# Expert loop of a mixture layer: another order of the operand splits, of the loads, and of the release of v and w tiles

## The chip, the cores and the metric

The kernel runs on one core of one Trainium2 chip. The metric is the time of one execution on the device in microseconds (us). Beside TensorE (PE) the core has VectorE (DVE), ScalarE (ACT), GpSimd (POOL) and SyncE (SP), which here only issues loads and stores. Each engine runs its own list of instructions in order; they wait for each other on counting semaphores.

## The reference

An encoder of two layers for 512 tokens of width 1024. A layer is a token mixer, a cross attention and a retrieval feed-forward (peer_ffn), which is the part that the change touches. It picks, for each token and each of 8 heads, 16 out of 16384 experts; an expert is one row of peer_u and one of peer_v:

```python
u = peer_u[eb]
a = jax.nn.gelu(jnp.einsum('thkd,td->thk', u, xb).astype(jnp.float32))
wgt = (a * gb).astype(xb.dtype)
return jnp.einsum('thk,thkd->td', wgt, peer_v[eb])
```

## The kernel before

For three of the four 128-token tiles (DENSE, DTOK = 384 tokens) the kernel does not gather. It computes every expert densely, with a gate that is zero for experts that a token did not choose. The 16384 experts are 128 tiles of 128; `expert_stage` goes over them in 32 groups of GROUP = 4 (e = 0 to 3). The program's text is expanded once and run for each of the two layers. The last token tile does gather: GpSimd fetches 128 rows of peer_u and of peer_v at a time, four of each per group, and VectorE does their products (row_product, row_output).

All dense products are done as three float32r matmuls (`mm3`, lines 123 to 125): high part by high part, low by high and high by low. So each tile of weights or gates has to be split: ScalarE copies it to the rounded high part ("hi", u_hi, v_hi, w_hi) and VectorE subtracts that from the raw tile (the low part "lo", u_lo, v_lo, w_lo).

One group, by engine:

- TensorE: for each e the first product (24 matmuls over 8 chunks of the width, tile A0 to A3 in this text) of u tile e with the 384 tokens, into bank 2 + e % 2. It waits for the low part (`ulo`) and for the gelu that freed the bank (`ge`). Then the second product, twice 36 matmuls: half 0 gives columns 0 to 511, half 1 columns 512 to 1023, in each half e = 0 to 3, and for each e three token tiles; it sums over all four experts in six banks, and counts `om` as each is done.
- ScalarE, for each e: v_hi e, u_hi of the next but one tile, gelu e, w_hi e. v_hi 0 of a group waits until the second product of the group before is wholly done (`om`, line 1971). After the four, the gelu of the four row products.
- VectorE, for each e: v_lo e, u_lo, multiplication by the gates (`exp_w<-exp_w,exp_gates`, line 2027), w_lo e. Then four row products (L1999), the row weights, two row outputs (L2007), three additions of the output banks of half 0 to the residual (L2014), two row outputs, three additions of half 1.
- SyncE, for each e: the load of u tile n + 2 once u_lo n is done, of v tile n + 2 once v_lo n is done, of the gates n + 2 once the multiplication n is done (line 1884, `ahead`). The raw buffers ur, vr and gt hold two tiles each (slot e % 2). uh and ul too hold two tiles, vh, vl, wh and wl hold the four of a group. In the first two groups stores of gates of the last block stand between the loads (`store_gates`).

A semaphore's wait in the same list holds back all that stands behind it on that engine. That is what sets the order of the work here: nothing is scheduled by a program, all is written out.

Of the kernel before, what the change touches and what calls it, by code (L numbers as in the profile page):

```python
# [18 lines left out]
ALU = mybir.AluOpType  # L19
# [22 lines left out]
GROUP = 4  # L42
# [1762 lines left out]
def expert_stage(nc, res, U, V, last_block, SL, u_rows, v_rows, l):  # L1805
# [7 lines left out]
    with Stage(nc, "exp") as st:  # L1813
# [31 lines left out]
        ad = st.sem("output_bank_added")  # L1845
        rd = st.sem("row_products_summed")
# [7 lines left out]
        def _(sp):  # L1854
# [29 lines left out]
            def ahead(g, e, last):  # L1884
                n = g * GROUP + e
                sp.wait_ge(ulo, n + 1)
                load_u(0 if last and e >= GROUP - 2 else n + 2, e % 2)
                if not (last and e >= GROUP - 2):
                    sp.wait_ge(vlo, n + 1)
                    load_v(n + 2, e % 2)  # L1890
                    sp.wait_ge(wo, n + 3)
                    load_g(n + 2, e % 2)

            for n in range(FIRST):
                if n == GROUP:

                    sp.wait_ge(g_out, 32)
                ahead(n // GROUP, n % GROUP, False)
                store_gates(n + 1)
            sp.wait_ge(g_out, 16 * (FIRST + 1))  # L1900
            with sp.Fori(FIRST // GROUP, NG - 1) as g:
                for e in range(GROUP):
                    ahead(g, e, False)
            for e in range(GROUP):
                ahead(NG - 1, e, True)
# [21 lines left out]
        def _(pe):  # L1927
            pe.sem_inc(am, 1)
            pe.sem_inc(om, 1)
            with pe.Fori(0, NG) as g:  # L1930
# [9 lines left out]
                for half in range(2):  # L1940
                    cols = slice(half * CHUNK, (half + 1) * CHUNK)
                    for e in range(GROUP):
# [3 lines left out]
                        for t in range(DENSE):  # L1946
# [5 lines left out]
                            if e == GROUP - 1:  # L1952
                                i.then_inc(om, 1)

        @b.scalar
        def _(act):
# [7 lines left out]
            u_hi(1, 1)  # L1964
            with act.Fori(0, NG) as g:
                for e in range(GROUP):
                    n = g * GROUP + e
                    act.wait_ge(v_in[e % 2], g * 32 + (e // 2) * 16 + 16)
                    if e == 0:

                        act.wait_ge(om, g * NO + 1)
                    act.copy(vh[:, e], vr[:, e % 2]).then_inc(vho, 1)  # L1972
                    if e:
                        act.wait_ge(am, n + 1)
                        u_hi(n + 1, (e + 1) % 2)
                    act.wait_ge(am, n + 2)
                    act.wait_ge(wlo, n + 1)
                    act.activation(w[:, e % 2], PS[:, 2 + e % 2, 0:DTOK], ACT.Gelu_apprx_tanh).then_inc(ge, 1)  # L1978
                    act.wait_ge(wo, n + 3)
                    act.copy(wh[:, e], w[:, e % 2]).then_inc(who, 1)  # L1980
# [328 lines left out]
```

## Time and profile before

| | us |
|---|---|
| median of three runs | 5006.38 |
| lowest, highest | 5004.93, 5008.29 |
| the profiled execution, its own time | 5007.78 |
| its span | 5006.0 |
| TensorE busy | 4198.0 (84%) |
| VectorE busy | 3155.8 (63%) |
| ScalarE busy | 1736.2 (35%) |

The page gives busy time and the costliest groups of instructions with the idle time of the engine in front of them and what ended it. The expert loops of the two layers run from about 1285 to 2500 us and from about 3775 to 4990 us of the span. Within them the work repeats from group to group, so a timeline of one group, with start times in us from the span's start, is the most telling view; the windows show the granted TensorE clock (1.00 is 2.4 GHz, 0.50 is 1.2 GHz) and what the transfer engines move.

### The profile page before, as it was taken

The page shows a single profiled execution, that of the slowest core. Times are in us where ns is not written, and L with a number is a line of the kernel's source. Part 1 is how long each engine was busy: PE and PEld are TensorE (multiplying, and loading weights), DVE is VectorE, ACT ScalarE, POOL GpSimd, SP SyncE. Part 2 cuts the span into 40 slices and gives each one's busy share as a digit, 9 for nine tenths or more (in the row PEclk, how much of TensorE's full clock was granted, in tenths as well). Part 3 has the DMA queues.
Part 4 walks back from the last instruction along what each step waited for, and adds up shares of the span by engine and source line. Part 5 has one row for each costly group of instructions (what it writes and reads, how often), then busy time and mean ns, then how long its engine had stood idle before and what let it go on. Part 6 is the DMA issues. An engine that isn't in the chain of part 4 may idle for free. (4 is left out here: it accounts for less than half of the span.)

```text
span 5006.0 us, 64200 instructions
## 1 busy us (share of the span) xinstructions
PE 4198.0 (84%) x21706; PEld 3734.1 (75%) x21706; DVE 3155.8 (63%) x5125; ACT 1736.2 (35%) x2506; POOL 1391.9 (28%) x992
## 2 busy tenths in 40 slices
PE   8869798646799999999897797886467999999997
PEld 6669677546688888888776796775466888888887
DVE  3464334599677777777735543336896777777776
ACT  2242222109543343333322322221094334334333
POOL 0143101155322322322201531112553232232231
PEclk9989899879899999999998898998798999999999
DMA  3100212105877777777531003120058777777775
GB/s 116 47 9 1 101 59 72 34 1 131 249 261 244 242 251 242 251 246 243 198 104 42 9 1 110 64 67 26 1 140 270 247 245 251 244 247 249 239 249 196
DMA packets 458568, 750.34 MB, mean 150 GB/s; under 512 B 241232, under 2 KB 278864, under 8 KB 458192
## 3 DMA queue, kind: packets, MB, share of 16 engines
q1 hardware_dynamic: 384720, 480.40, 29.5%
q0 software_dynamic: 73728, 268.47, 15.8%
q8 instruction: 60, 0.98, 0.1%
q14 instruction: 60, 0.49, 0.0%
HBM read 696.35 MB, written 52.43 MB: 150 GB/s over the span
## 5 line engine op out<-in xcount | busy, mean ns | idle before, releaser
L123 PE MATMUL banks<-act_hi,exp_uT_hi 128*128 128x384 f32 x2048 | 742.8, 363 | 183.6 <-DVE exp_uT_lo L1994 183.6
L1913 POOL DMA_INDIRECT exp_u_gathered<-in_peer_u,row_experts x256 | 390.3, 1525 | 1601.3 <-DVE exp_row_a L1999 1532.3
L124 PE MATMUL banks<-act_hi,exp_uT_lo 128*128 128x384 f32 x2048 | 732.7, 358 | 0.0
L125 PE MATMUL banks<-act_lo,exp_uT_hi 128*128 128x384 f32 x2048 | 732.4, 358 | 0.0
L124 PE MATMUL banks<-exp_v_hi,exp_w_lo 128*128 128x512 f32 x1536 | 598.4, 390 | 0.0
L123 PE MATMUL banks<-exp_v_hi,exp_w_hi 128*128 128x512 f32 x1536 | 598.1, 389 | 0.0
L125 PE MATMUL banks<-exp_v_lo,exp_w_hi 128*128 128x512 f32 x1536 | 597.7, 389 | 0.0
L123 PEld LDWEIGHTS banks<-act_hi,exp_uT_hi 128*128 128x128 f32 x2048 | 416.2, 203 | 208.1 <-DVE exp_uT_lo L1994 205.6
L124 PEld LDWEIGHTS banks<-act_hi,exp_uT_lo 128*128 128x128 f32 x2048 | 416.4, 203 | 2.4
L125 PEld LDWEIGHTS banks<-act_lo,exp_uT_hi 128*128 128x128 f32 x2048 | 415.2, 203 | 0.0
L1972 ACT CAST exp_v_hi<-exp_v_raw 128x1024 fp32r<-128x1024 f32 x256 | 268.0, 1047 | 355.1 <-PE banks L125 354.7
L2027 DVE TENSOR_TENSOR exp_w<-exp_w,exp_gates 128x384 f32<-128x384 f32 x256 | 142.0, 555 | 357.3 <-ACT exp_w L1978 335.2
L1994 DVE TENSOR_TENSOR exp_uT_lo<-exp_uT_raw,exp_uT_hi 128x1024 fp32r<-128x1024 f32 x260 | 317.2, 1220 | 72.5 <-ACT exp_uT_hi L1961 72.3
L2022 DVE TENSOR_TENSOR exp_v_lo<-exp_v_raw,exp_v_hi 128x1024 fp32r<-128x1024 f32 x256 | 313.0, 1223 | 78.1 <-ACT exp_v_hi L1972 78.1
L2007 DVE SCALAR_TENSOR_TENSOR residual<-exp_v_gathered,exp_row_w,residual 128x1024 f32<-128x1024 f32 x256 | 328.2, 1282 | 15.6
L125 PEld LDWEIGHTS banks<-exp_v_lo,exp_w_hi 128*128 128x128 f32 x1536 | 288.4, 188 | 60.4
L123 PEld LDWEIGHTS banks<-exp_v_hi,exp_w_hi 128*128 128x128 f32 x1536 | 288.3, 188 | 58.2
L124 PEld LDWEIGHTS banks<-exp_v_hi,exp_w_lo 128*128 128x128 f32 x1536 | 288.3, 188 | 57.7
L1913 POOL DMA_INDIRECT exp_v_gathered<-in_peer_v,row_experts x256 | 285.4, 1115 | 84.3 <-issue 75.9
L1725 DVE TENSOR_TENSOR gate_one_hots<-slot_keys,iota 128x1024 f32<-128x1024 f32 x192 | 296.8, 1619 | 3.0 <-DVE row_experts L1689 1.7
L1999 DVE CUSTOM_DVE_ANT_0 exp_u_gathered<-exp_u_gathered,rows 128x1024 f32<-128x1024 f32 x256 | 298.5, 1222 | 0.0
L1748 PE MATMUL banks<-gate_one_hots,gate_gated_one_hots 128*128 128x128 f32 x1536 | 205.7, 289 | 101.7 <-POOL gate_gated_one_hots L1735 79.8
(386 smaller groups left out, 8295.8 us busy)
## 6 DMA issues: line engine op xcount, KB each, us to landing
exp_uT_raw<-in_peer_uT SPq DMA_DIRECT2D x260, 512.0 KB, 4.2
exp_v_raw<-in_peer_v SPq DMA_DIRECT2D x256, 512.0 KB, 4.3
exp_gates<-dense_gates SPq DMA_DIRECT2D x256, 192.0 KB, 2.7
win_project_raw<-in_w_in SPq DMA_DIRECT2D x32, 1024.0 KB, 5.5
dense_gates<-gate_block SPq DMA_DIRECT2D x6, 4096.0 KB, 20.7
wkv_project_raw<-in_w_xkv SPq DMA_DIRECT2D x16, 1024.0 KB, 5.0
wpq_project_raw<-in_peer_wq SPq DMA_DIRECT2D x16, 1024.0 KB, 5.1
dense_gates<-last_gates SPq DMA_DIRECT2D x4, 4096.0 KB, 20.7
```

What stands on the lines that cost most here:

```text
L123: pe.matmul(out, lhs[0], rhs[0], start=first, stop=False)
L124: pe.matmul(out, lhs[1], rhs[0], start=False, stop=False)
L125: return pe.matmul(out, lhs[0], rhs[1], start=False, stop=last)
L1725: dve.tensor_tensor(oh[:, q], SL.idx[:, :, bass.ds(first(it, q), SUB)][:, :, :, None].broadcast_to(shape), res.iota[:, None, None, :].broa ...
L1748: i = pe.matmul(PS[:, q, k * P:(k + 1) * P], gh[:, q, k, :], oh[:, q, 0, k, :], start=True, stop=True)
L1913: pool.indirect_dma_start(out, None, table, bass.IndirectOffsetOnAxis(SL.row_idx[:, slot:slot + 1], 0)).then_inc(done, 16)
L1972: act.copy(vh[:, e], vr[:, e % 2]).then_inc(vho, 1)
L1994: dve.tensor_tensor(ul[:, slot], ur[:, slot], uh[:, slot].bitcast(F32), ALU.subtract).then_inc(ulo, 1)
L1999: dve.tensor_tensor_reduce(out=gu[:, e], in0=gu[:, e], in1=SL.rows[:], scale=1.0, scalar=0.0, op0=ALU.mult, op1=ALU.add, accum_out=ra[:, e ...
L2007: dve.scalar_tensor_tensor(out=X[:, DENSE, :], in0=gv[:, e], scalar=rw[:, e:e + 1], in1=X[:, DENSE, :], op0=ALU.mult, op1=ALU.add).then_in ...
L2022: dve.tensor_tensor(vl[:, e], vr[:, e % 2], vh[:, e].bitcast(F32), ALU.subtract).then_inc(vlo, 1)
L2027: dve.tensor_tensor(w[:, e % 2], w[:, e % 2], gt[:, e % 2], ALU.mult).then_inc(wo, 1)
```

## The change

Five things are moved; no computation is added or left out.

1. ScalarE and VectorE do the u parts of tile n + 2 as the first thing after tile n of the first product is done, in front of the gelu.
2. TensorE counts a new semaphore `vw` when expert e (0 to 2) is done in the second half of the second product. ScalarE's v_hi 0, 1 and 2 wait for that instead of for the end of the whole product; v_hi 3 waits for the end. v_hi 0 and 1 move in front of the group's first gelu, v_hi 2 and 3 stand between gelu 0 and w_hi 0 and between gelu 1 and w_hi 1.
3. w_hi and w_lo of an expert follow the v parts of a later one.
4. SyncE's loads are listed in another order, and the loads of u tiles 2 and 3 stand in front of the loop.
5. On VectorE the first row product stands between the multiplication by gates and w_lo of expert 2.

The diff, cut to the lists and functions:

```diff
+        vw = st.sem("v_and_w_used")
...
-            def ahead(g, e, last):
-                n = g * GROUP + e
+            def u_after(n, slot, dummy=False):
                 sp.wait_ge(ulo, n + 1)
-                load_u(0 if last and e >= GROUP - 2 else n + 2, e % 2)
-                if not (last and e >= GROUP - 2):
-                    sp.wait_ge(vlo, n + 1)
-                    load_v(n + 2, e % 2)
-                    sp.wait_ge(wo, n + 3)
-                    load_g(n + 2, e % 2)
-
-            for n in range(FIRST):
-                if n == GROUP:
+                load_u(0 if dummy else n + 2, slot)
+
+            def v_after(n, slot):
+                sp.wait_ge(vlo, n + 1)
+                load_v(n + 2, slot)
+
+            def g_after(n, slot):
+                sp.wait_ge(wo, n + 3)
+                load_g(n + 2, slot)
+
+            def ahead(g, last, stores):
+                n = g * GROUP
+                v_after(n + 0, 0)
+                v_after(n + 1, 1)
+                for e in range(GROUP):
+                    if e == GROUP - 1 and not last:
+                        g_after(n + e, e % 2)
+                    if not last or e < 2:
+                        u_after(n + e + 2, e % 2, last)
+                    if e < GROUP - 1 and (not last or e < 2):
+                        g_after(n + e, e % 2)
+                    if e + 2 < GROUP and (not last or e + 2 < 2):
+                        v_after(n + e + 2, (e + 2) % 2)
+                    if stores:
+                        store_gates(n + e + 1)
+
+            u_after(0, 0)
+            u_after(1, 1)
+            for g in range(FIRST // GROUP):
+                if g == 1:
 
                     sp.wait_ge(g_out, 32)
-                ahead(n // GROUP, n % GROUP, False)
-                store_gates(n + 1)
+                ahead(g, False, True)
...
-                for e in range(GROUP):
-                    ahead(g, e, False)
-            for e in range(GROUP):
-                ahead(NG - 1, e, True)
+                ahead(g, False, False)
+            ahead(NG - 1, True, False)
...
+            pe.sem_inc(vw, GROUP - 1)
...
@@ -1951,6 +1970,8 @@
                                     (vh[:, e, cols], vl[:, e, cols]), e == 0, e == GROUP - 1)
                             if e == GROUP - 1:
                                 i.then_inc(om, 1)
+                            elif half == 1 and t == DENSE - 1:
+                                i.then_inc(vw, 1)
...
+            def v_hi(g, e):
+                act.wait_ge(v_in[e % 2], g * 32 + (e // 2) * 16 + 16)
+                act.copy(vh[:, e], vr[:, e % 2]).then_inc(vho, 1)
+
+            def gelu(n, e):
+                act.wait_ge(am, n + 2)
+                act.wait_ge(wlo, n + 1)
+                act.activation(w[:, e % 2], PS[:, 2 + e % 2, 0:DTOK], ACT.Gelu_apprx_tanh).then_inc(ge, 1)
+
+            def w_hi(n, e):
+                act.wait_ge(wo, n + 3)
+                act.copy(wh[:, e], w[:, e % 2]).then_inc(who, 1)
+
             with act.Fori(0, NG) as g:
-                for e in range(GROUP):
-                    n = g * GROUP + e
-                    act.wait_ge(v_in[e % 2], g * 32 + (e // 2) * 16 + 16)
+                n = g * GROUP
+                for e in range(2):
+                    act.wait_ge(vw, g * (GROUP - 1) + e + 1)
+                    v_hi(g, e)
+                for e in range(GROUP - 1):
+                    act.wait_ge(am, n + e + 2)
+                    u_hi(n + e + 2, e % 2)
+                    gelu(n + e, e)
                     if e == 0:
-
+                        act.wait_ge(vw, g * (GROUP - 1) + GROUP - 1)
+                        v_hi(g, 2)
+                    if e == 1:
                         act.wait_ge(om, g * NO + 1)
-                    act.copy(vh[:, e], vr[:, e % 2]).then_inc(vho, 1)
-                    if e:
-                        act.wait_ge(am, n + 1)
-                        u_hi(n + 1, (e + 1) % 2)
-                    act.wait_ge(am, n + 2)
-                    act.wait_ge(wlo, n + 1)
-                    act.activation(w[:, e % 2], PS[:, 2 + e % 2, 0:DTOK], ACT.Gelu_apprx_tanh).then_inc(ge, 1)
-                    act.wait_ge(wo, n + 3)
-                    act.copy(wh[:, e], w[:, e % 2]).then_inc(who, 1)
-                act.wait_ge(am, g * GROUP + GROUP + 1)
-                u_hi(g * GROUP + GROUP + 1, 1)
-                act.wait_ge(rd, g * GROUP + GROUP)
+                        v_hi(g, 3)
+                    w_hi(n + e, e)
+                gelu(n + GROUP - 1, GROUP - 1)
+                u_hi(n + GROUP + 1, 1)
+                w_hi(n + GROUP - 1, GROUP - 1)
+                act.wait_ge(rd, n + GROUP)
...
+            def v_lo(n, e):
+                dve.wait_ge(vho, n + 1)
+                dve.tensor_tensor(vl[:, e], vr[:, e % 2], vh[:, e].bitcast(F32), ALU.subtract).then_inc(vlo, 1)
+
+            def gated(g, n, e):
+                dve.wait_ge(ge, n + 3)
+                dve.wait_ge(g_in[e % 2], g * 32 + (e // 2) * 16 + 16)
+                dve.tensor_tensor(w[:, e % 2], w[:, e % 2], gt[:, e % 2], ALU.mult).then_inc(wo, 1)
+
+            def w_lo(n, e):
+                dve.wait_ge(who, n + 1)
+                dve.tensor_tensor(wl[:, e], w[:, e % 2], wh[:, e].bitcast(F32), ALU.subtract).then_inc(wlo, 1)
+
             with dve.Fori(0, NG) as g:
-                for e in range(GROUP):
-                    n = g * GROUP + e
-                    dve.wait_ge(vho, n + 1)
-                    dve.tensor_tensor(vl[:, e], vr[:, e % 2], vh[:, e].bitcast(F32), ALU.subtract).then_inc(vlo, 1)
-                    if e:
-                        u_lo(n + 1, (e + 1) % 2)
-                    dve.wait_ge(ge, n + 3)
-                    dve.wait_ge(g_in[e % 2], g * 32 + (e // 2) * 16 + 16)
-                    dve.tensor_tensor(w[:, e % 2], w[:, e % 2], gt[:, e % 2], ALU.mult).then_inc(wo, 1)
-                    dve.wait_ge(who, n + 1)
-                    dve.tensor_tensor(wl[:, e], w[:, e % 2], wh[:, e].bitcast(F32), ALU.subtract).then_inc(wlo, 1)
-                u_lo(g * GROUP + GROUP + 1, 1)
-                row_product(g, 0)
-                row_product(g, 1)
-                row_product(g, 2)
-                row_product(g, 3)
+                n = g * GROUP
+                v_lo(n, 0)
+                v_lo(n + 1, 1)
+                for e in range(GROUP - 1):
+                    u_lo(n + e + 2, e % 2)
+                    gated(g, n + e, e)
+                    if e < 2:
+                        v_lo(n + e + 2, e + 2)
+                    else:
+                        row_product(g, 0)
+                    w_lo(n + e, e)
+                gated(g, n + GROUP - 1, GROUP - 1)
+                u_lo(n + GROUP + 1, 1)
+                w_lo(n + GROUP - 1, GROUP - 1)
+                for e in range(1, GROUP):
+                    row_product(g, e)
```

What stands in a row on ScalarE (exp_uT is u, exp_v is v, exp_w the gelu's output). At the beginning of a group's gelu 0, before:

```order
L1978 ACT_TABLE_LOAD
L1978 ACTIVATE exp_w<-banks 128x384
...
L1980 CAST exp_w_hi<-exp_w 128x384
L1972 CAST exp_v_hi<-exp_v_raw 128x1024
...
L1961 CAST exp_uT_hi<-exp_uT_raw 128x1024
```

The same place on ScalarE after the change, from the two v_hi that now open the group:

```order
L1988 CAST exp_v_hi<-exp_v_raw 128x1024
L2002 REGISTER_ALU
L1988 CAST exp_v_hi<-exp_v_raw 128x1024
...
L1982 CAST exp_uT_hi<-exp_uT_raw 128x1024
L1992 REGISTER_ALU
L1993 ACT_TABLE_LOAD
L1993 ACTIVATE exp_w<-banks 128x384
...
L1988 CAST exp_v_hi<-exp_v_raw 128x1024
L1996 REGISTER_ALU
L1997 CAST exp_w_hi<-exp_w 128x384
L1982 CAST exp_uT_hi<-exp_uT_raw 128x1024
```

The u copy of tile 2 stood fifth, behind the table load, the gelu, w_hi 0 and v_hi 1; it stands before the table load now, and v_hi 2 and w_hi 0 stand between gelu 0 and the u copy of tile 3.

VectorE at the beginning of a group, before:

```order
L2022 TENSOR_TENSOR exp_v_lo<-exp_v_raw,exp_v_hi 128x1024
L2025 REGISTER_ALU
L2026 ISA
L2027 TENSOR_TENSOR exp_w<-exp_w,exp_gates 128x384
L2029 TENSOR_TENSOR exp_w_lo<-exp_w,exp_w_hi 128x384
L2021 REGISTER_ALU
L2022 TENSOR_TENSOR exp_v_lo<-exp_v_raw,exp_v_hi 128x1024
L1994 TENSOR_TENSOR exp_uT_lo<-exp_uT_raw,exp_uT_hi 128x1024
```

And after:

```order
L2055 TENSOR_TENSOR exp_v_lo<-exp_v_raw,exp_v_hi 128x1024
L2028 REGISTER_ALU
L2029 TENSOR_TENSOR exp_uT_lo<-exp_uT_raw,exp_uT_hi 128x1024
L2059 ISA
L2060 TENSOR_TENSOR exp_w<-exp_w,exp_gates 128x384
L2055 TENSOR_TENSOR exp_v_lo<-exp_v_raw,exp_v_hi 128x1024
L2064 TENSOR_TENSOR exp_w_lo<-exp_w,exp_w_hi 128x384
L2028 REGISTER_ALU
L2029 TENSOR_TENSOR exp_uT_lo<-exp_uT_raw,exp_uT_hi 128x1024
```

The first row here is v_lo 1. u_lo 2 follows it at once, where it stood behind the multiplication, w_lo 0 and v_lo 1; u_lo 3 stands behind v_lo 2 and w_lo 0.

SyncE in one pass of the loop (the ISA row ahead of a load is its wait), after the change; before it was u, v, gates four times:

```order
L1860 DMA exp_v_raw<-in_peer_v 128x1024
L1860 ISA
L1860 DMA exp_v_raw<-in_peer_v 128x1024
L1857 ISA
L1857 DMA exp_uT_raw<-in_peer_uT 128x1024
L1863 ISA
L1863 DMA exp_gates<-dense_gates 128x384
L1860 ISA
L1860 DMA exp_v_raw<-in_peer_v 128x1024
```

Two v loads, on v_lo 0 and v_lo 1, now open the pass; the u loads of tiles 2 and 3 that stood there have gone to the end of the pass before and ahead of the loop.

## Rows read from the trace of the kernel before

**Rows 1.** The page: busy time; costliest group (busy, mean ns, idle before, releaser).
```profile
PE 4198.0 (84%) x21706; PEld 3734.1 (75%) x21706; DVE 3155.8 (63%) x5125; ACT 1736.2 (35%) x2506; POOL 1391.9 (28%) x992
...
L123 PE MATMUL banks<-act_hi,exp_uT_hi 128*128 128x384 f32 x2048 | 742.8, 363 | 183.6 <-DVE exp_uT_lo L1994 183.6
```

**Rows 2.** ScalarE timeline (start us, us, operation): row gelu, groups 0 and 31.
```profile
1334.87 0.20 ACT L1984 ACTIVATE exp_row_gelu<-exp_row_a 128x4 f32<-128x4 f32 x1 [5.87 <-DVE exp_row_a L1999]
...
2487.13 0.20 ACT L1984 ACTIVATE exp_row_gelu<-exp_row_a 128x4 f32<-128x4 f32 x1 [5.87 <-DVE exp_row_a L1999]
...
3826.92 0.21 ACT L1984 ACTIVATE exp_row_gelu<-exp_row_a 128x4 f32<-128x4 f32 x1 [5.87 <-DVE exp_row_a L1999]
...
4979.24 0.21 ACT L1984 ACTIVATE exp_row_gelu<-exp_row_a 128x4 f32<-128x4 f32 x1 [5.87 <-DVE exp_row_a L1999]
```

**Rows 3.** TensorE timeline of one group [idle before <-releaser].
```profile
1808.48 0.40 PE L123 MATMUL banks<-exp_v_hi,exp_w_hi 128*128 128x512 f32 x1
...
1824.84 0.34 PE L123 MATMUL banks<-act_hi,exp_uT_hi 128*128 128x384 f32 x1
...
1833.15 0.33 PE L125 MATMUL banks<-act_lo,exp_uT_hi 128*128 128x384 f32 x1
...
1835.76 0.44 PE L123 MATMUL banks<-act_hi,exp_uT_hi 128*128 128x384 f32 x1 [2.28 <-DVE exp_uT_lo L1994]
```

**Rows 4.** Windows, TensorE alone: window, length, busy, granted clock, DMA share, GB/s.
```profile
1838.40:1839.40 1.00, 1.00 (x5) 0.50 0.85 317
```

**Rows 5.** Windows: busy by engine (instructions), granted clock, DMA share, GB/s.
```profile
40.00:160.00 120.00, 120.00 (x515) 96.50 (x514) 40.56 (x34) 19.59 (x11) 0.00 (x0) 1.00 0.30 96
1340.00:1420.00 80.00, 75.43 (x367) 68.95 (x366) 59.77 (x76) 30.55 (x40) 25.04 (x20) 0.96 0.86 283
1420.00:2480.00 1060.00, 993.78 (x4782) 904.48 (x4781) 770.08 (x993) 413.41 (x547) 296.09 (x224) 0.96 0.72 246
```

**Rows 6.** ScalarE timeline: a table load at the layer's start, then one group's beginning.
```profile
1290.42 1.04 ACT L1961 CAST exp_uT_hi<-exp_uT_raw 128x1024 fp32r<-128x1024 f32 x1 [2.38 <-DMA exp_uT_raw<-in_peer_uT]
1291.48 1.28 ACT L1972 ACT_TABLE_LOAD   x1
...
1825.04 1.05 ACT L1972 CAST exp_v_hi<-exp_v_raw 128x1024 fp32r<-128x1024 f32 x1 [5.95 <-PE banks L125]
1829.34 1.28 ACT L1978 ACT_TABLE_LOAD   x1 [3.25 <-PE banks L125]
1830.64 0.49 ACT L1978 ACTIVATE exp_w<-banks 128x384 f32<-128x384 f32 x1
...
1832.27 1.05 ACT L1972 CAST exp_v_hi<-exp_v_raw 128x1024 fp32r<-128x1024 f32 x1
1833.22 1.03 ACT L1961 CAST exp_uT_hi<-exp_uT_raw 128x1024 fp32r<-128x1024 f32 x1
```

**Rows 7.** VectorE timeline, end of one group and beginning of the next.
```profile
1811.51 1.23 DVE L1994 TENSOR_TENSOR exp_uT_lo<-exp_uT_raw,exp_uT_hi 128x1024 fp32r<-128x1024 f32 x1 [0.40 <-ACT exp_uT_hi L1961]
...
1824.86 1.88 DVE L2014 TENSOR_TENSOR residual<-banks,residual 128x512 f32<-128x512 f32 x3
1826.66 1.22 DVE L2022 TENSOR_TENSOR exp_v_lo<-exp_v_raw,exp_v_hi 128x1024 fp32r<-128x1024 f32 x1
...
1833.35 1.22 DVE L2022 TENSOR_TENSOR exp_v_lo<-exp_v_raw,exp_v_hi 128x1024 fp32r<-128x1024 f32 x1 [0.39 <-ACT exp_v_hi L1972]
1834.49 1.22 DVE L1994 TENSOR_TENSOR exp_uT_lo<-exp_uT_raw,exp_uT_hi 128x1024 fp32r<-128x1024 f32 x1
```

**Rows 8.** SyncE queue timeline: the group's first v load.
```profile
1828.10 0.33 SPq L1859 DMA_DIRECT2D exp_v_raw<-in_peer_v  x1
```

**Rows 9.** Landing: that load; v loads, 1420 to 2430; u loads, 1340 to 1420.
```profile
DMA to landing us min/median/max: 5.3/5.3/5.3
...
DMA to landing us min/median/max: 3.1/4.3/5.6
...
DMA to landing us min/median/max: 3.3/5.7/8.1
```

## Prediction

> **What bounds the kernel now.** I read the page first. TensorE is busy 84% of the span, and in front of the first product of the expert loop it has waited 183.6 us, all for VectorE's u_lo at L1994 [rows 1]. So the loop is held by TensorE, with a hole that belongs to the u tiles.
>
> Next, the length of a group. The row gelu stands once per group of four experts; from group 0 to group 31 it moves 2487.13 - 1334.87 = 1152.26 us in layer 1 and 1152.32 us in layer 2, so 31 groups take 37.17 us each [rows 2].
>
> Next, what TensorE needs. Its timeline shows the second product from 1808.48 to 1824.84, without a hole: 16.36 us. Then two tiles of the first product, whose last matmul starts at 1833.15; with one spacing of 0.177 us (8.48 us for 48 matmuls) they take 8.48 us, 4.24 us a tile. The third tile starts only at 1835.76, after 2.28 us of waiting for u_lo [rows 3]. Four tiles and the second product at this pace are 4 x 4.24 + 16.36 = 33.32 us. The remaining 37.17 - 33.32 = 3.85 us are the wait (2.3 to 2.5 us) and a spell at half clock that follows it: in 1838.4 to 1839.4 the granted clock is 0.50, 1.2 instead of 2.4 GHz [rows 4]. Over the loop it averages 0.96, while in 120 us of projection in which TensorE never idles it is 1.00 [rows 5]. I therefore count the spell as a consequence of the wait.
>
> **Why u is late before.** In each group's timelines, tile A0 ends 4.24 after the group's start and ScalarE reacts at 4.50 (1829.34). But it then does the table load, gelu 0, w_hi 0, v_hi 1 and only then u_hi 2, at 1833.22, 8.4 us after the group's start [rows 6]. u_lo 2 starts at 1834.49 behind v_lo 1, and TensorE goes on 1.27 later [rows 7, 3].
>
> **The change part by part.** I walk the new orders with t = 0 at a group's first matmul, and TensorE at full clock: A0 to A3 start at 0, 4.24, 8.48, 12.72, the second product at 16.96; its second half at 25.14, and that half's experts 0, 1, 2 end at 27.2, 29.2, 31.3.
>
> 1. u first (releases tile A2). u_hi 2 at 4.50. u_lo starts 1.08 after a hi copy (v_hi 1832.27 to v_lo 1833.35, [rows 6, 7]): 5.58; TensorE may go at 5.58 + 1.27 = 6.85. A2 is due at 8.48: 1.6 us spare, the wait of 2.3 is gone. What is late next? A2 also needs gelu 0 out of its bank. The table load now stands behind u_hi: 4.50 + 1.05 = 5.55, gelu at 5.55 + 1.30 = 6.85 (1829.34 to 1830.64), done 7.34: 1.1 spare.
>
> 2. v_hi 0 and 1 in the preceding group's second half, on their experts' release (27.2 and 29.2), while ScalarE before sits idle until the output is done (5.95 us at 1825.04, [rows 6]). Cost nothing; their table load goes there too. Their lo parts stay behind the last three output additions on VectorE. Those now wait for TensorE: the last bank is done at 33.5, so the third addition starts at 0.25 of the next group and v_lo 0 at 0.85 (an addition takes 1.88 / 3), v_lo 1 at 2.0.
>
> 3. The queue. SP issues the load of v 2 1.44 after v_lo starts (1826.66 to 1828.10, [rows 7, 8]): 2.3. It lands 5.3 later by the single row, 5.6 at most in 1420 to 2430 [rows 9]: 7.6 to 7.9. ScalarE wants it for v_hi 2 behind gelu 0, at 7.25, so v_hi 2 starts at 7.6. Behind it on ScalarE stand w_hi 0 (8.55) and u_hi 3 (9.0; A1 ends at 8.48, seen at 8.74). On VectorE: v_lo 2 at 8.7, w_lo 0 at 9.85, u_lo 3 at 10.4; TensorE may go at 11.7. A3 is due at 12.72: 1.0 spare. This is the tightest place. The load may land up to 6.3 us after its issue before TensorE waits at all. The other loads have more: v 3 is issued at 3.4 and wanted at 10.4; u 4 at 7.0, wanted at 13.0; u 5 at 11.8, wanted at 17.6. The waits in SP's new list (v_lo 0, v_lo 1, u_lo 2, w 0, v_lo 2, u_lo 3, w 1, ...) fulfil in that order, so none is queued behind a later one.
>
> 4. Second half of the loop on VectorE. Before, from the last u_lo (1811.51) to the last addition group (1824.86) is 13.35 us [rows 7]. After, A3 is done at 16.96, gelu 3 starts at 17.2, u_hi 5 at 17.6, u_lo 5, the last, at 18.7; one row product less (1.14, the spacing of 1024-column operations at 1833.35 and 1834.49) and a w_lo more (384 columns, 0.5 as an estimate from that) stand behind it: ready for the last additions at 31.4, when their first bank is done at 32.1. w_lo 3 starts near 19.9 and the second product's expert 3 begins at 23.1. So VectorE has 0.7 us left per group, and no wait for TensorE here.
>
> 5. DMA volume is the same, 9.17 MB a group (sixteen tiles of 512 KB, 192 KB of gates four times): 246 GB/s now at a share of 0.72, 275 GB/s then. In 1340 to 1420, with gate stores beside, the queues carried 283 GB/s at 0.86 [rows 5]. It fits, with little over.
>
> The increments of vw ride on existing matmuls. The added waits are ScalarE's, on counts that are raised before it comes (2.0 us before the group's end at the latest for v_hi 2). I take 0. No row prices a wait that is already met; nothing makes it a gain, and as a loss it has to exceed the 1.0 us of spare of step 3 before TensorE notices: 0.1 us a group, 6 us, is my bound.
>
> **Sum.** 3.85 x 31 = 119.4 us a layer. At the layer's end the last additions end 0.85 us after the last matmul instead of 1.9 (1824.86 + 1.88): 1.1. Group 0 waits for its first gates as before: 0, between -2 and +3. Two layers: 2 x 120.5 = 241 us. The profiled run is 5007.8, 1.4 above the median of 5006.4; 5006.4 - 241 gives 4766 (and 4767 for a profiled one).
>
> **Rivals.**
> (a) A smaller wait takes the old one's place at A2 or A3. What speaks for it: 1.0 and 1.1 us of spare on chains of six steps. The table load now comes right behind a copy, where it was behind an idle wait of 3.25 us. At the layer's start it also stands behind a copy, at 1291.48 after 1290.42 + 1.04, and costs nothing extra [rows 6]. Bounds for an extra drain: 0 by that row, above one more load, 1.28 us, as far as rows go. With the latter gelu 0 is done at 8.62 and A2 waits 0.2 us a group: 62 x 0.2 = 12, 4778; if every such wait brought the slow spell (about 1.6 us) too, 62 x 1.8 = 112, 4878.
> The Trainium skill (ScalarE: Activation LUTs, What ACT_TABLE_LOAD costs) puts a switch of set at about 2.66 us, load and drain together; the trace here has 1.28 and no drain. By the page gelu 0 would end as late as under the upper bound, give or take 0.1 us, and the time would be the one just worked out from rows.
> (b) The queues give out. v 2 lands later than 6.3 us after issue. For it: u loads took up to 8.1 us at 283 GB/s, behind gate stores [rows 9]. Against: the stores are gone after two groups, and the gathers of v rows, which a row output releases, get further from this load: row outputs 2 and 3 ended with the group (1824.86, [rows 7]) and the load came 3.3 later; now they end at 31.4, 1.9 before the group's end, and the load comes at 2.3, so 4.2 later. At 8.1 us A3 is 1.8 late, plus the spell: 62 x 3.4 = 211, 4977.
> (c) The slow spell is not a consequence of the wait: 62 x (3.85 - 2.4) = 90 stay, 4856. Against it stand the 120 us at 1.00.
> (d) Slower than before: v_hi 2 blocks ScalarE, with u_hi 3 behind it. From landings over 6.3 + 3.85 - 1.6 = 8.6 us on (spell included) a group is longer than 37.17; at 9.5 us 62 x 0.9 = 56 more, 5062. No v load took that long in 1420 to 2430.
> (e) The change doesn't do what it says: ScalarE comes late to u_hi 2, for instance held at the loop's top by v_hi 1. Then nothing moves, 5006. Against: by the walk that tile's load is issued 17 us before v_hi 0 wants it (10.2 and 27.2).
>
> **How the numbers follow.** Forecast 0.74; (a) 0.10, (b) 0.05, (c) 0.04, (d) 0.03, (e) 0.04. The forecast is 4766. Its own range, from group 0, the cost of waits and 0.1 us a group, is 4756 to 4776. To leave out no more than 2 in 10, the range takes in (a) and (c): 4756 to 4878. About 0.2% (10 us) is what a measurement can tell from no change. Faster 0.93, same 0.04, slower 0.03.
>
> **What would show it.** The row gelus 33.3 us apart; granted clock 1.00 inside the loop; TensorE's wait for u_lo at the first product below 30 us in all, in the layers' first groups; u_hi 2 at 4.5, u_lo 3 near 10.4; v_hi 2 released by its load, near 7.6; loop at 275 GB/s. Wrong would be: a wait before every fourth tile with v_hi 2 starting beyond 8.6 (b, d); a hole before the third with gelu 0 later than 8 (a); clock dips without holes (c).

## The result, and the profile after

| | before | after |
|---|---|---|
| median, 4 runs each | 5005.66 us | 4765.98 us |
| lowest, highest | 5003.36, 5008.29 | 4762.16, 4767.08 |
| ratio, 95% interval | | 0.952 (0.9503 to 0.9536) |
| span of the profiled execution | 5006.0 | 4764.2 |

The changed kernel is faster by 240 us; 241 were forecast. The page of its profile (busy time, and the costliest group as in [rows 1]: busy, mean ns, idle before, releaser):

```profile
PE 4097.4 (86%) x21706; PEld 3654.1 (77%) x21706; DVE 3147.7 (66%) x5125; ACT 1729.5 (36%) x2506; POOL 1352.9 (28%) x992
...
L123 PE MATMUL banks<-act_hi,exp_uT_hi 128*128 128x384 f32 x2048 | 699.4, 341 | 43.9 <-ACT exp_w L1993 23.9
```

The idle time in front of the first product fell from 183.6 to 43.9 us; 20.0 of it, in 4 waits, is still for u_lo, and the other 23.9 is for the gelu. The mean of one such matmul fell too, from 363 to 341 ns, since the half-clock spells of the steady groups are gone. The window of the loop, as the last of [rows 5] (busy by engine, clock, DMA share, GB/s):

```profile
1420.00:2330.00 910.00, 910.00 (x4589) 832.27 (x4588) 738.22 (x960) 390.24 (x519) 270.76 (x218) 1.00 0.84 276
```

In 910 us TensorE has no hole and is at full clock throughout, while the transfer engines move 276 GB/s where they moved 246.

The timeline of one group follows; its first matmul is at 1807.23, and times into the group count from there. ScalarE:

```profile
1801.36 1.28 ACT L1988 ACT_TABLE_LOAD   x1 [3.48 <-PE banks L125]
1802.65 2.00 ACT L1988 CAST exp_v_hi<-exp_v_raw 128x1024 fp32r<-128x1024 f32 x2
1811.73 1.05 ACT L1982 CAST exp_uT_hi<-exp_uT_raw 128x1024 fp32r<-128x1024 f32 x1 [7.07 <-PE banks L125]
1812.80 1.28 ACT L1993 ACT_TABLE_LOAD   x1
1814.09 0.49 ACT L1993 ACTIVATE exp_w<-banks 128x384 f32<-128x384 f32 x1
1814.48 1.04 ACT L1988 CAST exp_v_hi<-exp_v_raw 128x1024 fp32r<-128x1024 f32 x1
...
1815.89 1.05 ACT L1982 CAST exp_uT_hi<-exp_uT_raw 128x1024 fp32r<-128x1024 f32 x1
```

VectorE in the same group (the last additions of the group before, then v_lo 0 and 1, u_lo 2, u_lo 3, and the last u_lo):

```profile
1806.05 2.05 DVE L2049 TENSOR_TENSOR residual<-banks,residual 128x512 f32<-128x512 f32 x3 [0.78 <-PE banks L125]
1808.02 2.35 DVE L2055 TENSOR_TENSOR exp_v_lo<-exp_v_raw,exp_v_hi 128x1024 fp32r<-128x1024 f32 x2
1812.81 1.23 DVE L2029 TENSOR_TENSOR exp_uT_lo<-exp_uT_raw,exp_uT_hi 128x1024 fp32r<-128x1024 f32 x1 [2.44 <-ACT exp_uT_hi L1982]
...
1817.16 1.22 DVE L2029 TENSOR_TENSOR exp_uT_lo<-exp_uT_raw,exp_uT_hi 128x1024 fp32r<-128x1024 f32 x1
...
1825.83 1.23 DVE L2029 TENSOR_TENSOR exp_uT_lo<-exp_uT_raw,exp_uT_hi 128x1024 fp32r<-128x1024 f32 x1 [0.38 <-ACT exp_uT_hi L1982]
```

The queue's two v loads there, and how long the first of them took to land:

```profile
1809.49 1.49 SPq L1860 DMA_DIRECT2D exp_v_raw<-in_peer_v  x2
...
DMA to landing us min/median/max: 4.8/4.8/4.8
```

u_hi 2 starts at 4.50 us into the group and the table load stands behind it; the gelu follows 1.29 after the load's start. v_hi 2 comes at 7.25, straight behind the gelu, with no wait for its load.

ScalarE's row gelus, as in [rows 2], of group 3 and of group 31 of the first layer:

```profile
1431.15 0.20 ACT L2019 ACTIVATE exp_row_gelu<-exp_row_a 128x4 f32<-128x4 f32 x1 [4.78 <-DVE exp_row_a L2034]
...
2364.11 0.20 ACT L2019 ACTIVATE exp_row_gelu<-exp_row_a 128x4 f32<-128x4 f32 x1 [4.78 <-DVE exp_row_a L2034]
```

From 1431.15 to 2364.11 there are 28 steps of 33.32 us. Group 2 is longer: from its first matmul to group 3's it takes 37.16 us (35.10 in the second layer). The waits in each layer that are left behind its first matmul are at A2 of group 0 and at A3 of group 2. TensorE in the first layer (A2 of group 0, then group 2's first matmul, its A3, and group 3's first matmul):

```profile
1310.64 0.66 PE L123 MATMUL banks<-act_hi,exp_uT_hi 128*128 128x384 f32 x1 [11.57 <-ACT exp_w L1993]
...
1370.21 0.34 PE L123 MATMUL banks<-act_hi,exp_uT_hi 128*128 128x384 f32 x1
...
1385.14 0.53 PE L123 MATMUL banks<-act_hi,exp_uT_hi 128*128 128x384 f32 x1 [2.05 <-DVE exp_uT_lo L2029]
...
1407.37 0.34 PE L123 MATMUL banks<-act_hi,exp_uT_hi 128*128 128x384 f32 x1
```

### The profile page after: what moved, and what is told of

Read it like the earlier page. It is cut to its first block and busy times, and to the rows that moved or that the text cites. A ratio compares the mean times of both kernels' runs of the same rounds, so it can differ in the third digit from the quotient of the medians.

```text
span 4764.2 us, 64232 instructions
## 1 busy us (share of the span) xinstructions
PE 4097.4 (86%) x21706; PEld 3654.1 (77%) x21706; DVE 3147.7 (66%) x5125; ACT 1729.5 (36%) x2506; POOL 1352.9 (28%) x992
## 5 line engine op out<-in xcount | busy, mean ns | idle before, releaser
L123 PE MATMUL banks<-act_hi,exp_uT_hi 128*128 128x384 f32 x2048 | 699.4, 341 | 43.9 <-ACT exp_w L1993 23.9
L1931 POOL DMA_INDIRECT exp_u_gathered<-in_peer_u,row_experts x256 | 324.0, 1266 | 1357.1 <-DVE exp_row_a L2034 1305.3
L124 PE MATMUL banks<-act_hi,exp_uT_lo 128*128 128x384 f32 x2048 | 697.9, 341 | 0.0
L125 PE MATMUL banks<-act_lo,exp_uT_hi 128*128 128x384 f32 x2048 | 697.8, 341 | 0.0
L1982 ACT CAST exp_uT_hi<-exp_uT_raw 128x1024 fp32r<-128x1024 f32 x260 | 272.8, 1049 | 531.4 <-PE banks L125 488.0
L123 PEld LDWEIGHTS banks<-act_hi,exp_uT_hi 128*128 128x128 f32 x2048 | 388.0, 189 | 48.1 <-DVE exp_uT_lo L2029 45.7
L124 PEld LDWEIGHTS banks<-act_hi,exp_uT_lo 128*128 128x128 f32 x2048 | 388.0, 189 | 2.4
L125 PEld LDWEIGHTS banks<-act_lo,exp_uT_hi 128*128 128x128 f32 x2048 | 387.9, 189 | 0.0
L1931 POOL DMA_INDIRECT exp_v_gathered<-in_peer_v,row_experts x256 | 312.2, 1220 | 132.2 <-DVE residual L2042 72.4
L2049 DVE TENSOR_TENSOR residual<-banks,residual 128x512 f32<-128x512 f32 x384 | 251.5, 687 | 48.3 <-PE banks L125 48.3
```

The lines of the kernel that those rows point to most:

```text
L123: pe.matmul(out, lhs[0], rhs[0], start=first, stop=False)
L124: pe.matmul(out, lhs[1], rhs[0], start=False, stop=False)
L125: return pe.matmul(out, lhs[0], rhs[1], start=False, stop=last)
L1931: pool.indirect_dma_start(out, None, table, bass.IndirectOffsetOnAxis(SL.row_idx[:, slot:slot + 1], 0)).then_inc(done, 16)
L1982: act.copy(uh[:, slot], ur[:, slot]).then_inc(uho, 1)
L2049: dve.tensor_tensor(x, PS[:, OUT[half][t], :], x, ALU.add).then_inc(ad, 1)
```

## The experiments

Every kernel here is measured beside the kernel before on the same chip. e1 to e5 are one execution each, and the time of before is given with each; e8, e9 and e10 are medians of 4 or 5.

### Which part carries the gain

**e1: the tile-by-tile release undone.** The changed kernel, but v_hi 0, 1 and 2 wait for the whole second product.

```diff
             with act.Fori(0, NG) as g:
                 n = g * GROUP
+                act.wait_ge(om, g * NO + 1)
                 for e in range(2):
-                    act.wait_ge(vw, g * (GROUP - 1) + e + 1)
                     v_hi(g, e)
```

> The changed kernel with the tile-by-tile release undone: v_hi 0, 1 and 2 wait for the whole second product again, u parts first and the new queue stay. My theory (the release only buys landing time for the load of v 2): v_hi 0 begins 1.5 us into the group behind its table load instead of 4.6 us before it, v_lo 0 at 2.6, the load of v 2 is issued at 4.0 instead of 2.3 and lands near 8.7 to 9.3; u_lo 3 starts at 11.5 to 12.0 and the fourth tile of the first product waits 0.1 to 0.6 us. Group of 33.4 to 33.9 us, 4772 to 4803 us in all, up to 100 us more if such a short wait brings the half-clock spell. Rival (the release is what carries the gain): a group of over 36 us, 4930 us or more.

Measured: 4767.56 us (before 5008.51), groups of 33.32. Nothing is lost, and TensorE waits nowhere between 1420 and 2300. The rows of one group, with its first matmul at 1806.63; ScalarE, then the queue, then the landing of the first load:

```profile
1808.18 2.00 ACT L1984 CAST exp_v_hi<-exp_v_raw 128x1024 fp32r<-128x1024 f32 x2
1811.13 1.05 ACT L1978 CAST exp_uT_hi<-exp_uT_raw 128x1024 fp32r<-128x1024 f32 x1 [0.96 <-PE banks L125]
...
1813.97 1.05 ACT L1984 CAST exp_v_hi<-exp_v_raw 128x1024 fp32r<-128x1024 f32 x1
...
1810.74 1.49 SPq L1859 DMA_DIRECT2D exp_v_raw<-in_peer_v  x2
...
DMA to landing us min/median/max: 3.2/3.2/3.2
```

The v copies fit between the group's start and u_hi 2, with 0.96 us to spare. The v load leaves 4.11 us into the group instead of 2.26, but it lands in 3.2 us instead of 4.8, at 7.3; and v_hi 2 isn't late. That landing is what the expectation had wrong: it took 4.7 to 5.3 us for it, and so a short wait at A3 and 4772 us at least. The release brings nothing that a single execution can tell (1.6 us between this one and the changed kernel's median).

**e2: the old queue.** The changed kernel with SyncE's list of before (u, v, gates four times).

```diff
-            def ahead(g, last, stores):
-                n = g * GROUP
-                v_after(n + 0, 0)
-                v_after(n + 1, 1)
...
+            def ahead(g, e, last):
+                n = g * GROUP + e
+                sp.wait_ge(ulo, n + 1)
+                load_u(0 if last and e >= GROUP - 2 else n + 2, e % 2)
+                if not (last and e >= GROUP - 2):
+                    sp.wait_ge(vlo, n + 1)
+                    load_v(n + 2, e % 2)
+                    sp.wait_ge(wo, n + 3)
+                    load_g(n + 2, e % 2)
```

> The changed kernel with the old queue alone: SyncE again issues u, v, gates for each expert in turn, so the load of u 3 stands behind the gates' wait of expert 0. My theory (the queue is needed, since the u parts now want their tiles earlier): u 3 is issued at 8.7 us of the group instead of in the group before and lands at 13, the fourth tile waits 2.6 us; u 4 and u 5 come late too and hold w_hi 3, which the second product's last expert waits for by some 4 us. Group of 40 to 44 us, 5180 to 5430 us in all, slower than the kernel before. Rival (the queue hardly matters, since tiles are loaded two ahead): 33.3 to 34 us a group, 4766 to 4810.

Measured: 5346.18 us (before 5008.51), slower than the kernel before by 338. Groups in the loop take about 40 to 44 us. The waits of TensorE in 1420 to 2300 (us, times, longest):

```profile
PE banks L123 <- DVE exp_w_lo L2047: 70.8, 29, 4.1
PE banks L123 <- DVE exp_uT_lo L2012: 42.4, 21, 2.7
```

And the cause, in the queue and on ScalarE:

```profile
1800.31 0.33 SPq L1863 DMA_DIRECT2D exp_gates<-dense_gates  x1
1800.90 0.33 SPq L1857 DMA_DIRECT2D exp_uT_raw<-in_peer_uT  x1
...
1804.69 1.05 ACT L1965 CAST exp_uT_hi<-exp_uT_raw 128x1024 fp32r<-128x1024 f32 x1 [3.90 <-DMA exp_uT_raw<-in_peer_uT]
```

A u load stands behind the gates' load, which waits for the multiplication. The tile's buffer has long been free, and ScalarE waits for such a load three times in this group (3.90, 3.47 and 3.98 us).

**e3: the u parts last.** The new queue (the u load behind gates and v) and the tile-by-tile release, but u_hi and u_lo behind w_hi and w_lo, on ScalarE and VectorE.

```diff
                 for e in range(GROUP - 1):
-                    act.wait_ge(am, n + e + 2)
-                    u_hi(n + e + 2, e % 2)
                     gelu(n + e, e)
...
                     w_hi(n + e, e)
+                    u_hi(n + e + 2, e % 2)
```

> The changed kernel with the u parts moved behind w_hi and w_lo of the expert (queue in the order of that release), release tile by tile kept. My theory (u first is what removes the wait): u_hi 2 starts at 8.4 us instead of 4.5, u_lo 2 at 9.7, the third tile waits 2.5 us, the fourth does not; the half-clock spell is back. Group of 36 to 37.4 us, 4930 to 5020 us. Rival (the early v parts alone suffice, since they take the v copy out of the way): under 34 us a group, below 4810.

Measured: 4981.42 us (before 5008.51); most groups take 36.9 to 38.3 us, some 35.2 to 35.9. TensorE waits for u_lo at A2 again:

```profile
1832.62 0.53 PE L123 MATMUL banks<-act_hi,exp_uT_hi 128*128 128x384 f32 x1 [2.82 <-DVE exp_uT_lo L2026]
...
PE banks L123 <- DVE exp_uT_lo L2026: 54.6, 24, 3.2
```

**e4: the u parts first, and nothing else.** The kernel before with only the new order of u_hi and u_lo.

```diff
                     act.wait_ge(am, n + 2)
+                    if e < GROUP - 1:
+                        u_hi(n + 2, e % 2)
                     act.wait_ge(wlo, n + 1)
                     act.activation(...)
```

> The kernel before with one part alone: u_hi of the next but one tile in front of the gelu and u_lo in front of the gates' multiplication; v parts, release and queue as before. My theory: the load of u 3 still stands in the queue behind the gates of expert 0, so ScalarE now sits in front of u_hi 3 with the gelu behind it; group of 40 to 44 us, 5180 to 5430 us, slower than before. Rival (u first alone carries the gain): 33.3 to 34 us a group, 4766 to 4810.

Measured: 5313.84 us (before 5008.51), groups of 39.4 to 44 us. ScalarE waits for u loads, as in e2. This one was issued at 1825.75, 0.60 behind the issue of a gates load:

```profile
1829.31 1.05 ACT L1961 CAST exp_uT_hi<-exp_uT_raw 128x1024 fp32r<-128x1024 f32 x1 [2.83 <-DMA exp_uT_raw<-in_peer_uT]
```

**e9: the two together, without the rest.** The kernel before with e4's order and a queue in the order of release. The v parts stay in their own expert's place, v_hi 0 waits for the whole product, and the row products stay where they were.

```diff
+                for e in range(GROUP):
+                    if not last or e < 2:
+                        sp.wait_ge(vlo, n + e + 1)
+                        load_v(n + e + 2, e % 2)
+                        if e < GROUP - 1:
+                            u_after(n + e + 2, e % 2, last)
+                        sp.wait_ge(wo, n + e + 3)
+                        load_g(n + e + 2, e % 2)
+                        if e == GROUP - 1:
+                            u_after(n + e + 2, 1, last)
```

> The kernel before with the u parts first and the queue in the order of release, and nothing of the v and w parts moved: v_hi 0 and 1 are made in their own expert's group and wait for the whole second product. Theory (order and queue carry the whole gain; the tile-by-tile release and the place of the v parts bring nothing): ScalarE makes v_hi 0 at the second product's end, u_hi 2 at 4.5 us into the group, the gelu is done at 7.3, u_hi 3 at 9.4 and u_lo 3 at 10.7, so TensorE needs no wait; groups of 33.3 us, clock 1.00 in the loop, 4766 us (4760 to 4790). Rival (the v parts have to be made beforehand): u_lo 3 or a w_lo comes late, TensorE waits in each group, groups over 34 us, 4810 or more.

Measured: 4765.76 us median of 4 (before 5007.2), ratio 0.9516 (0.9501 to 0.953). In total that is the whole gain. Window of the loop, then ScalarE in a group whose first matmul is at 1804.68:

```profile
1420.00:2300.00 880.00, 880.00 (x4433) 803.94 (x4432) 712.56 (x929) 375.91 (x502) 283.38 (x211) 1.00 0.84 275
...
1804.88 1.05 ACT L1980 CAST exp_v_hi<-exp_v_raw 128x1024 fp32r<-128x1024 f32 x1 [5.55 <-PE banks L125]
1809.20 1.05 ACT L1969 CAST exp_uT_hi<-exp_uT_raw 128x1024 fp32r<-128x1024 f32 x1 [3.27 <-PE banks L125]
```

The totals agree, but not every group does. Group 2 takes 33.32 us here, in both layers, where the changed kernel has 37.16 and 35.10: its first v load leaves 3.69 us into the group instead of 7.37. Group 0 of the first layer takes 50.81 here and 48.88 in the changed kernel. The reasons for either were not traced.

So of the five things that the change moves, two carry the gain, and only together: the order alone costs 305 us (5313.84 against 5008.51), a new queue without the order (e3, which has the release as well; the two were not separated) gives 27, order and queue give 241. With u first, a u tile's buffer is free and wanted earlier, and the old list of the queue then holds its load behind a wait for something later.

### How near the edge the change runs, and what a wait costs

**e5: padding in front of u_hi 2.** The changed kernel with 2, 3, 4 or 5 copies of 128 by 512 on ScalarE (1.92 us for 3, 2.58 for 4, 3.23 for 5), each chained to the one before. They do nothing for the result. A row of several copies covers all of them, and u_hi 2 starts 0.1 before its end.

```diff
                     act.wait_ge(am, n + e + 2)
+                    if e == 0:
+                        for j in range(5):
+                            act.wait_ge(pd, g * 5 + j + 1)
+                            act.copy(pad[:], SL.rows[:, 0:CHUNK]).then_inc(pd, 1)
                     u_hi(n + e + 2, e % 2)
```

> The changed kernel with two idle copies of 128x512 on ScalarE in front of u_hi 2 in each group (they write a tile that nobody reads). They shift u_hi 2, the table load and gelu 0 by about 1.2 us. Theory: the spare at the third tile is 1.1 us, so TensorE waits 0.1 us there or not at all; group 33.3 to 33.5 us, 4766 to 4778; clock 1.00. Rival (the order has no such spare, the chain was just in time): group longer by the 1.2 us, 4840.

> Three such copies, shift about 1.9 us. Theory: the third tile waits for gelu 0 by 0.8 us a group (4815); if a wait of 0.8 us brings the half-clock spell as the old one of 2.3 us did, 1.6 us more a group (4915). Rival (the spell doesn't depend on the wait): no spell, clock 1.00.

> Four such copies, shift about 2.6 us. Theory: the third tile waits 1.5 us a group (4859 by the wait alone, 4958 with a spell of 1.6 us in each group). Rival (spell independent of the wait): no spell.

> Five such copies, shift about 3.2 us. Theory: the third tile waits 2.1 us a group, nearly as long as in the kernel before, and the granted clock falls to 0.50 for some 3 us a group as there: 4896 by the wait alone, 4995 with the spell. Rival (the spell came from another cause of the old order): 4896 at a clock of 1.00 in the loop.

| copies | us (before 5011.14) | A2's listed wait for gelu 0, us | most groups, us | clock, 1420 to 2300 |
|---|---|---|---|---|
| 2 | 4776.65 | none | 33.58 | 1.00 |
| 3 | 4812.33 | 0.62 | 34.16 | 1.00 |
| 4 | 4858.16 | 1.35 | 34.89 | 1.00 |
| 5 | 4972.15 | 2.00 | 37.07, every fourth 35.55 | 0.97 |

With 2, 3 and 4 copies the times are those expected from the wait alone. With 5, the time lies between the two values expected, 4896 without a spell at half clock and 4995 with one in each group.

The rows of one group with 4 copies (its first matmul, the padding, u_hi 2, A2), then A2 with 5 copies:

```profile
1824.47 0.34 PE L123 MATMUL banks<-act_hi,exp_uT_hi 128*128 128x384 f32 x1
...
1828.98 2.58 ACT L2012 COPY exp_pad<-rows 128x512 f32<-128x512 f32 x4 [7.07 <-PE banks L125]
1831.46 1.04 ACT L1985 CAST exp_uT_hi<-exp_uT_raw 128x1024 fp32r<-128x1024 f32 x1
...
1834.45 0.42 PE L123 MATMUL banks<-act_hi,exp_uT_hi 128*128 128x384 f32 x1 [1.35 <-ACT exp_w L1996]
...
1823.36 0.48 PE L123 MATMUL banks<-act_hi,exp_uT_hi 128*128 128x384 f32 x1 [2.00 <-ACT exp_w L1996]
```

The padding shifts u_hi 2 by 2.48 us (1828.98 to 1831.46). A2 starts 9.98 into the group (1824.47 to 1834.45) where it was due at 8.48, so it is 1.50 late, and the spare of gelu 0 at A2 is 2.48 - 1.50 = 0.98. The same count gives 1.05 with 3 copies and 0.98 with 5; 1.1 was forecast. The listed wait is smaller than the loss each time: groups grow by 0.84 with 0.62 listed and by 1.57 with 1.35. Most of that difference is in how the view counts. It lets a matmul of 0.34 us end before the idle time begins, while the next one would have followed after 0.177 (the spacing in [rows 3]). That is also why 2 copies lengthen a group by 0.26 with no wait listed.

With a listed wait of 2.00 us most groups grow by 3.75. A window behind such a wait is at half clock (1.2 GHz), where one behind the wait of 1.35 is at full clock (2.4 GHz):

```profile
1826.00:1827.00 1.00, 1.00 (x5) 1.00 (x4) 1.00 (x2) 0.84 (x1) 0.00 (x0) 0.51 0.69 196
...
1836.00:1838.00 2.00, 2.00 (x13) 2.00 (x12) 2.00 (x3) 1.93 (x3) 0.00 (x0) 1.00 0.78 256
```

Every fourth group of the last kernel takes 35.55, 2.23 above 33.32. Its wait is the same 2.00 us, and the clock behind it stays at 1.00 (1496 to 1498, for instance). A hole of that size thus has a spell behind it in three groups of four, and the spell itself costs 1.5 us.

### What is left at a layer's start

**e8: the start's queue.** In the changed kernel u 2 of group 0 is loaded behind a wait for the first store of gates, and group 2's loads behind a wait for all stores. Here both waits are moved behind the loads that don't need them.

```diff
+            store_gates(0)
             u_after(0, 0)
             u_after(1, 1)
+            sp.wait_ge(g_out, 16)
+            for n in range(2):
+                load_g(n, n)
...
+            ahead(FIRST // GROUP, False, False)
             sp.wait_ge(g_out, 16 * (FIRST + 1))
```

> The changed kernel with two edits at the layer's start: the loads of u 2 and u 3 are issued behind the first store of gates but ahead of the wait for it, and the wait for all stores of gates stands behind the third group's loads instead of ahead of them. Theory: in group 0 the third tile waited 11.6 us because u 2 was issued behind the 18 us wait for the store; u 2 now lands when the store is through, near 20 us after its issue, some 3 us earlier; in group 2 v 2 was issued 5 us late and the group took 36.5 us, now 33.3. Together 3 + 3.2 us a layer, 12 us in all: 4754 us. Rival (the loads only queue behind the store in the rings, and group 2's delay comes from slow stores, not from the wait): 4766, no change; or slower by up to 6 us where the early loads delay the first gates.

Measured: 4752.84 us median of 5 (before 5007.53), ratio 0.9492 (0.9479 to 0.9505), 13 us below the changed kernel; the executions of the two don't overlap (4749.46 to 4755.02, and 4762.16 to 4767.08). 4754 was expected. Group 2 takes 33.32, and group 0's wait is shorter by 4.25 us, where 3 were expected:

```profile
1304.45 0.66 PE L123 MATMUL banks<-act_hi,exp_uT_hi 128*128 128x384 f32 x1 [7.32 <-ACT exp_w L1993]
```

**e10: the first gathers behind the store.** The e8 kernel, in which GpSimd's gathers of a layer start when the first store of gates is done.

```diff
+            pool.wait_ge(g_out, 16)
             for g in range(SLOTS // GROUP):
```

> The e8 kernel, in which GpSimd's first gathers of a layer's first group also wait until the first store of the gates is done. Theory (that store, 16 to 18 us long, shares its DMA engines with eight 512 KB gathers and the first loads, and group 0's wait for its gelu, 7.3 us in e8, hangs on it): the store lands 6 to 12 us earlier, group 0's wait falls to 0 to 2 us, some 8 us a layer, 4730 to 4745 us. Rival (the store is slow by its own small pieces, whatever runs beside it): the wait stays at 7 us, 4753 us, or more if the row gathers come late for the row products.

Measured: 4753.47 us median of 5 (before 5007.2), no change from e8. The store's landing (KB each, median us), in the e8 kernel and then here:

```profile
dense_gates<-last_gates SPq DMA_DIRECT2D x1, 256.0 KB, 18.1
...
dense_gates<-last_gates SPq DMA_DIRECT2D x1, 256.0 KB, 7.6
```

The theory's first half holds: the gathers beside it more than double the store's time. Its second half fails. The wait at A2 of group 0 falls from 7.32 to 2.47 us, but another one appears. A later u load is now held 5.60 us in the queue, ScalarE waits for it, and TensorE waits in the second product:

```profile
1306.42 5.60 SPq L1857 DMA_DIRECT2D exp_uT_raw<-in_peer_uT  x1
...
1318.84 1.04 ACT L1983 CAST exp_uT_hi<-exp_uT_raw 128x1024 fp32r<-128x1024 f32 x1 [5.97 <-DMA exp_uT_raw<-in_peer_uT]
...
1321.66 0.80 PE L123 MATMUL banks<-exp_v_hi,exp_w_hi 128*128 128x512 f32 x1 [3.19 <-DVE exp_w_lo L2065]
```

Behind that wait there is a stretch at half clock: in 1320 to 1340 the granted clock is 0.83 here and 1.00 in e8. Together they make group 0 of the first layer 1.3 us longer than in e8 (46.26 and 44.96), although its waits add up to less. Whether the gathers, now later, are what holds that u load was not separated from the store of gates in front of it. The u load behind such a store is slow to leave the queue in the other kernels too (1.66 us at that place in e8, 4.67 behind the second store in the kernel before), where most loads take 0.33.

## Why the prediction was right, point by point

- **The frame holds.** 33.32 us for four tiles and the second product is what TensorE now takes, and the wait and its spell are gone in every group but group 2: that is the 3.85 x 31.
- **Step 1 holds.** u_hi 2 at 4.50; gelu 0 started at 6.86, forecast 6.85. Rival (a), an extra drain at the table load, is refuted: the gelu follows the load's start by 1.29. The Trainium skill (ScalarE: Activation LUTs, What ACT_TABLE_LOAD costs) adds 1.38 us of drain to a load of 1.28; the trace here shows the load and no drain. e5 puts the spare at 1.0 (1.1 forecast).
- **Step 2 is right in its times and wrong in its weight.** v_lo 0 came at 0.79 (0.85). But the walk let the release and the early v_hi stand as part of what buys the gain, and e1 and e9 show that they buy nothing in the total; group 2 is even without delay in e9. The prediction did not ask what the walk gives without them.
- **Step 3 is mis-sized on its landing, on the safe side.** The queue issued at 2.26 (2.3), but the load took 4.8, not 5.3, so v_hi 2 started at 7.25 without a wait (7.6 and released by its load), u_hi 3 at 8.66 (9.0), u_lo 3 at 9.93 (10.4). The spare before A3 was therefore 1.5, not 1.0. What rival (b) describes came about in group 2 alone, and by another way: not by a slow landing (v 2 took 3.6 us), but by a late issue, 7.37 us into the group, behind the wait for the last stores. v_hi 2 started at 10.96, 3.71 later than in a steady group. Less the 1.5 of spare, A3 had to be 2.2 late, and it was (1385.14 instead of 1382.93). The group grew by 3.84, so the spell took the other 1.6, as forecast. In the second layer A3 of group 2 was 1.7 late and the group grew by only 1.8: no spell.
- **Step 4 holds.** The last u_lo at 18.60 (18.7), and VectorE is ready 0.78 ahead of the first of the last three banks (0.7).
- **Step 5 holds.** 276 GB/s at a share of 0.84.
- **Rivals (c) and (e)** are refuted by the loop at clock 1.00 and by u_hi 2's time; e5 shows the spell coming back with a wait of 2.00 us and not with one of 1.35. **Rival (d)**'s way to slower was not seen, but e2 and e4 show one that the prediction didn't price: the u order without the queue.
- **The sum agrees with errors that cancel.** For layer 1, from the first matmul of group 1 to the last of the loop: 1154.03 us before (1340.34 to 2494.37), 1036.53 after (1336.89 to 2373.42). That is 117.5 instead of 119.4, since group 2 gave 3.8 back and before's groups were longer by 1.8 in all than I counted. Group 0, forecast at 0 (between -2 and +3), took 48.88 instead of 50.99 us: 2.1 gained (0.5 in layer 2), and the cause of it stays open. It also began 1.3 earlier in the span, and the tail gave 1.0 of its 1.1. So that 240 was met to within 1 us is in part luck. A slip of 1 us is in the sum itself: 5006.4 - 241 is 4765.4 and not 4766. The walk looked at steady groups only: it took group 2 for one of them, and did not see the queue's wait for the stores in front of group 2's loads, nor how much of group 0's wait could be had (e8).

The rows of group 2 on the queue (its first two v loads) and on ScalarE (v_hi 2):

```profile
1377.58 0.98 SPq L1860 DMA_DIRECT2D exp_v_raw<-in_peer_v  x2
...
1381.17 1.05 ACT L1988 CAST exp_v_hi<-exp_v_raw 128x1024 fp32r<-128x1024 f32 x1 [3.58 <-DMA exp_v_raw<-in_peer_v]
```

The rows of the count for layer 1: the first matmuls of groups 0 and 1 and the last of the loop, first of the kernel before, then of after:

```profile
1289.35 0.69 PE L123 MATMUL banks<-act_hi,exp_uT_hi 128*128 128x384 f32 x1 [8.29 <-DVE exp_uT_lo L1994]
...
1340.34 0.34 PE L123 MATMUL banks<-act_hi,exp_uT_hi 128*128 128x384 f32 x1
...
2494.37 0.39 PE L125 MATMUL banks<-exp_v_lo,exp_w_hi 128*128 128x512 f32 x1
...
1288.01 0.69 PE L123 MATMUL banks<-act_hi,exp_uT_hi 128*128 128x384 f32 x1 [8.24 <-DVE exp_uT_lo L2029]
...
1336.89 0.34 PE L123 MATMUL banks<-act_hi,exp_uT_hi 128*128 128x384 f32 x1
...
2373.42 0.39 PE L125 MATMUL banks<-exp_v_lo,exp_w_hi 128*128 128x512 f32 x1
```

## What to carry to other kernels

When work is moved forward on one engine, walk the queue that feeds it too: here the same order of splits costs 305 us with the old list of loads and saves 241 with a new one. A list of waits and loads should stand in the order in which its waits are fulfilled, and a wait for a rare event (a store) behind everything that doesn't need it. And before a change of several parts is credited, run it without each part: two of five parts carried this one, and one wait for a rare event, ahead of loads that do not need it, costs group 2 of the first layer 3.8 us.

## What the runs showed of the hardware that was not expected

- A listed wait of TensorE of 1.35 us left the clock at 1.00 and cost 1.57 us (e5, 4 copies). One of 2.00 us cost 3.75 in three groups of four, with a stretch at half clock behind it, and 2.23 without one in every fourth (5 copies). Group 2 of the changed kernel shows both as well: 2.05 listed cost 3.84 in the first layer, with the clock at 0.50 behind it (1386 to 1388), and 1.51 cost 1.78 in the second, at clock 1.00 (3759 to 3763). The prediction had priced a wait of 0.2 us with a spell at its upper bound, which no run bears out (3 copies: 0.62 of wait, 0.84 of loss).
- The same v load lands in 4.8 us when issued 2.26 us into the group and in 3.2 us when issued at 4.11 (e1). The shorter landing gave back 1.6 of the 1.85 us of delay. The last gather of v rows starts at 1806.38 in the changed kernel, 3.11 us ahead of that load, and at 1805.78 in e1, 4.96 ahead; such gathers land in 5.3 to 6.1 us. So more of them run beside the earlier load, which is the likely reason; it was not tested.
- A store of 256 KB took 18.1 us to land beside eight gathers and the first loads (e8), and 7.6 without the gathers (e10).
